# Seams of two attentions and a merge: who stores the last rows, which queues load the first ones, and the first tile in halves

## The chip, the cores and the metric

The kernel runs on one core of a Trainium2 chip. The time is device microseconds of one execution. TensorE (PE) multiplies, VectorE (DVE), ScalarE (ACT) and GpSimd (POOL) do the elementwise work, SyncE (SP) issues DMAs; ACT and POOL can issue them too.

## The reference

One block of an encoder, for 2048 tokens of width 1024, all in float32:

```
proj = x @ w_in                       # A: q k v, B: q k v, two gates
oa = swa_sink_attention(rope(aq), rope(ak), av, sinks)   # window of 2 chunks of 64, sink in the denominator
ob = diff_attention(rope(bq), rope(bk), bv, lam)         # (p1 - lam * p2) @ v, block-causal
ob = rms_norm(ob per head) * subln_g * (1 - lambda_init)
mix = (sig(gA) * (oa @ w_proj_a) + sig(gB) * (ob @ w_proj_b)) @ w_out
x = layer_norm(alpha * x + mix, ln1_g, ln1_b)
x = layer_norm(alpha * x + moe(x), ln2_g, ln2_b)         # 32 experts, 2 for each token
```

## The kernel before

The program is a row of phases: projection, differential attention (prefix `b_`, writes `ob`), window attention (`a_`, writes `oa`), merge (`m_`, writes `x1` and `acc`), routing, experts, final norm. Each phase has its own semaphores, and ends with a barrier of all engines; `Phase.__exit__` (L69) clears the semaphores and then has a second barrier. Lines L72 and L76 in the profile are these two. Nothing of a phase runs before the one ahead of it has ended on every engine. A product of two float32 matrices is made from high and low parts: ACT copies the high part, VectorE (or POOL) subtracts it to get the low part, and TensorE makes three products.

*Differential attention.* For each of 4 heads and 16 blocks of 128 queries, ACT scales the result to `parts`, POOL adds its two halves to `o` (L1056) and issues the store to `ob` (L1058). In between, TensorE makes the gates, which ACT stores (L1189). At its end POOL waits for its stores.

*Window attention.* 16 tiles of 128 queries, two units (key heads) each. TensorE makes the scores (L687 to L694), VectorE the maxima, ACT the exponentials, TensorE transposes and multiplies by the values. SP issues all loads in an order written out: `load_qk(0)`, `load_v(0)`, `load_qk(1)`, `load_v(1)`, and then in each tile those of two tiles ahead, with waits where a buffer must be free. `load_qk` has two halves, from `qk_hi` and `qk_lo`. For the first tile, which has no chunk before it, the keys are loaded in two pieces (L596 and L597). Beside all this POOL loads a slice of the merge's weights in each tile (`a_raw`, 512 KB, L666, two buffers), ACT makes its high and POOL its low part, and POOL adds the attention's two halves (L660).

*Merge.* 16 tiles of 128 tokens. SP loads `ln1_g`, `ln1_b`, `subln_g`, then `oin` (the rows of `oa` and `ob`), the gates and x of two tiles, and goes on two tiles ahead. VectorE makes the RMS norm of the `ob` half of `oin` (L1539 to L1547, with a square root on ACT, L1481, whose table has to be loaded first), TensorE transposes `oin` (L1430), ACT and VectorE split it (L1485, L1551), TensorE multiplies by `w_proj_a` (to `psa`) and `w_proj_b` (to `psb`), VectorE multiplies by the gates, POOL adds, TensorE transposes and multiplies by `w_out`. `norm` (L1553 to L1568) makes the layer norm up to (y - mean) / deviation, POOL multiplies by gamma and adds beta (L1518, L1520), and ACT stores the tile twice (L1500, L1501). Work is staged one and two tiles apart, in the order that `step` has for each engine.

## Time and profile before

| | |
|---|---|
| median of 3 runs | 2936.3 us (2932.4 to 2944.07) |
| profiled execution | 2936.18 us |
| its span | 2934.1 us |
| mean granted clock of TensorE | 0.949 |
| busy: PE, DVE, ACT, POOL | 89%, 57%, 38%, 29% |
| differential attention, first to last work | 480.6 to 1205 us |
| window attention | 1211.5 to 1383 us |
| merge | 1384.3 to 1802 us |
| DMAs issued by POOL: differential attention, window attention, experts | 64, 16, 100 |

The profile is of one execution. Busy time is the time in which an engine executed an instruction; a row of the timeline gives the start, the duration, the engine and line, and in brackets how long the engine had been idle and what ended that. Rows with a q behind the engine's name are of its instruction queue: DMA issues, waits, and DRAIN, in which the queue waits for its engine to have ended all that it began. The time from a DMA's issue to its landing is in the DMA view.

### The profile page before, as it was taken

To read this page: it belongs to the slowest core of one execution; us is meant where nothing else is said; L and a number is where in the kernel's file an instruction comes from. 1 tells how busy PE (TensorE), PEld (TensorE's weight loads), DVE (VectorE), ACT (ScalarE), POOL (GpSimd) and SP (SyncE) were. 2 spreads that over 40 slices of the span, in tenths; PEclk is the share of its full clock that TensorE was granted. 3 is DMA by queue.
4 is the path that set the end of the run, shared out by engine and by line. 5 is a ranking of instruction groups with operands and counts; after the bars stand their busy time and mean duration, and the time that the engine had idled before them with its cause. 6 is when DMAs were issued, how large, how long until landed. Compare 5 with 4: busy or idle time off the path is not lost. (4 is left out here: it accounts for less than half of the span.)

```text
span 2934.1 us, 45594 instructions
## 1 busy us (share of the span) xinstructions
PE 2611.3 (89%) x14634; PEld 2251.5 (77%) x14635; DVE 1677.0 (57%) x3050; ACT 1126.5 (38%) x1918; POOL 856.2 (29%) x653
## 2 busy tenths in 40 slices
PE   6999995999999999697899995499999999999970
PEld 5888884888888888687788884278888888888860
DVE  6333333666666666386344443576685557657748
ACT  3111111444454444365111111264574446646533
POOL 0111110101010010144122232155464445446535
PEclk9999997999999999798999998799999999999995
DMA  6344436665565653386333324378797779768846
GB/s 219 129 139 161 139 131 193 191 196 186 187 198 170 216 167 136 101 211 186 128 129 129 129 107 147 121 271 287 238 359 229 222 261 314 237 220 300 315 107 243
DMA packets 282227, 568.51 MB, mean 194 GB/s; under 512 B 44816, under 2 KB 140176, under 8 KB 280080
## 3 DMA queue, kind: packets, MB, share of 16 engines
q1 hardware_dynamic: 191184, 430.90, 43.3%
q0 software_dynamic: 18752, 65.02, 8.9%
q10 hardware_dynamic: 72192, 71.31, 7.2%
q8 instruction: 56, 0.92, 0.1%
q14 instruction: 43, 0.35, 0.0%
HBM read 435.55 MB, written 131.60 MB: 193 GB/s over the span
## 5 line engine op out<-in xcount | busy, mean ns | idle before, releaser
L1982 DVE TENSOR_TENSOR e_wl<-rw_raw,e_wh 128x1024 fp32r<-128x1024 f32 (+1 forms) x288 | 422.6, 1511 | 25.9 <-ACT e_wh L2132 25.9
L2132 ACT ACTIVATE e_wh<-rw_raw 128x1024 fp32r<-128x1024 f32 (+1 forms) x384 | 377.6, 1054 | 4.1 <-PE e_py L2097 4.1
L1982 POOL TENSOR_TENSOR e_wl<-rw_raw,e_wh 128x1024 f32 (+1 forms) x96 | 273.7, 2864 | 72.1 <-ACT e_wh L2132 72.1
L246 PE MATMUL j_pg<-qkv_w_hi,j_xh 128*128 128x512 f32 (+1 forms) x640 | 243.8, 381 | 9.0 <-DVE qkv_w_lo L416 9.0
L248 PE MATMUL j_pg<-qkv_w_lo,j_xh 128*128 128x512 f32 (+1 forms) x640 | 238.1, 372 | 0.0
L247 PE MATMUL j_pg<-qkv_w_hi,j_xl 128*128 128x512 f32 (+1 forms) x640 | 237.4, 371 | 0.0
L2083 PE MATMUL e_p_up<-e_wh,e_xh 128*128 128x256 f32 (+1 forms) x784 | 225.4, 287 | 0.0
L2085 PE MATMUL e_p_up<-e_wl,e_xh 128*128 128x256 f32 (+1 forms) x784 | 221.7, 283 | 0.0
L2084 PE MATMUL e_p_up<-e_wh,e_xl 128*128 128x256 f32 (+1 forms) x784 | 221.6, 283 | 0.0
L1056 POOL TENSOR_TENSOR b_o<-b_parts 128x128 f32<-128x128 f32 x64 | 31.2, 487 | 636.3 <-ACT b_parts L1173 636.3
L1107 PE MATMUL b_pg<-b_g_wh,b_g_xh 128*128 128x512 f32 x512 | 209.1, 408 | 0.7 <-DVE b_g_out L1294 0.7
L1107 PE MATMUL b_pg<-b_g_wl,b_g_xh 128*128 128x512 f32 x512 | 205.1, 401 | 0.0
L1107 PE MATMUL b_pg<-b_g_wh,b_g_xl 128*128 128x512 f32 x512 | 203.7, 398 | 0.0
L1238 DVE TENSOR_SCALAR_CACHE_REDUCE b_sc<-b_s 128x512 f32<-128x512 f32 (+3 forms) x320 | 179.2, 605 | 30.4 <-PE b_s L1079 18.6
L1164 ACT ACTIVATE b_th<-b_t 128x512 fp32r<-128x512 f32 (+3 forms) x160 | 85.4, 534 | 286.0 <-PE b_t L1092 277.3
L314 POOL TENSOR_TENSOR j_turned<-j_by_cos,j_by_sin 128x512 f32<-128x512 f32 x64 | 70.6, 1113 | 393.0 <-DVE j_by_sin L450 345.9
L1279 DVE TENSOR_TENSOR b_tl<-b_t,b_th 128x512 fp32r<-128x512 f32 (+3 forms) x160 | 97.5, 609 | 120.2 <-ACT b_th L1164 120.2
L2095 PE MATMUL e_py<-e_wh,e_hh 128*128 128x512 f32 x392 | 163.1, 416 | 0.0
L445 DVE TENSOR_TENSOR j_by_cos<-j_pg,qkv_cos 128x512 f32<-128x512 f32 x64 | 37.6, 588 | 216.5 <-DMA v_lo<-j_staged 145.8
L2083 PE MATMUL e_p_gate<-e_wh,e_xh 128*128 (+1 forms) x392 | 154.5, 394 | 5.9 <-DVE e_wl L1982 3.1
L1157 ACT ACTIVATE b_sc<-b_sc,b_nb 128x128 f32<-128x128 f32 (+15 forms) x128 | 153.2, 1197 | 6.9 <-DVE b_nb L1249 6.9
L2097 PE MATMUL e_py<-e_wl,e_hh 128*128 128x512 f32 x392 | 154.1, 393 | 0.0
(328 smaller groups left out, 7053.2 us busy)
## 6 DMA issues: line engine op xcount, KB each, us to landing
rw_raw<-w_gate_up SPq DMA_DIRECT2D x256, 512.0 KB, 6.1
rw_raw<-w_down SPq DMA_DIRECT2D x128, 512.0 KB, 8.5
b_g_xh<-xt_hi SPq DMA_DIRECT2D x64, 512.0 KB, 3.7
b_g_xl<-xt_lo SPq DMA_DIRECT2D x64, 512.0 KB, 4.9
gates<-b_g_out ACTq DMA_DIRECT2D x64, 256.0 KB, 5.2
m_gt<-gates SPq DMA_DIRECT2D x16, 1024.0 KB, 8.3
qk_hi<-j_staged ACTq DMA_DIRECT2D x16, 832.0 KB, 4.5
qk_lo<-j_staged ACTq DMA_DIRECT2D x16, 832.0 KB, 6.9
```

What stands on the lines that cost most here:

```text
L246: nc.tensor.matmul(out, xh[:, u, ks], w_hi[:, k, cs], start=(k == 0), stop=False)
L247: nc.tensor.matmul(out, xl[:, u, ks], w_hi[:, k, cs], start=False, stop=False)
L248: last = nc.tensor.matmul(out, xh[:, u, ks], w_lo[:, k, cs], start=False, stop=(k == KD - 1))
L1107: last = nc.tensor.matmul(pg[:], x_side, w_side, start=(q == 0), stop=(q == PASSES - 1))
L1238: nc.vector.tensor_scalar(sc[u][:, m, ks], bank[n % 4][:, 0:ks.stop - ks.start], 1.0, NEG, ALU.mult, ALU.max, accum_out=mx[:, u, m, g:g + ...
L1982: (nc.gpsimd if done is w_lo_pool else nc.vector).tensor_tensor(wl[:, slot(e, s), :], raw[:, s:s + 1, :], f(wh[:, slot(e, s), :]), ALU.sub ...
L2083: nc.tensor.matmul(out[:, 0:js.stop - js.start], xh[:, at], hi, start=(k == 0), stop=False)
L2084: nc.tensor.matmul(out[:, 0:js.stop - js.start], xl[:, at], hi, start=False, stop=False)
L2085: last = nc.tensor.matmul(out[:, 0:js.stop - js.start], xh[:, at], lo, start=False, stop=(k == KD - 1))
L2095: nc.tensor.matmul(py[:, js], hh[:, at], wh[:, n, js], start=(k == 0), stop=False)
L2097: last = nc.tensor.matmul(py[:, js], hh[:, at], wl[:, n, js], start=False, stop=(k == KF - 1))
L2132: nc.scalar.activation(wh[:, slot(e, s), :], raw[:, s:s + 1, :], ACT.Copy).then_inc(w_hi, 1)
```

## The change

There are four places.

1. In the differential attention the last of the 64 stores to `ob` is issued by SP, on a semaphore of its own, and not by POOL.
2. In the window attention the loads of the first tile's q and k are issued from two queues: the `qk_hi` half by SP, the `qk_lo` half by ACT, keys ahead of queries and the pieces needed for it ahead of the stand-in piece. The sinks are loaded behind them. POOL waits for the first scores before it loads the first slice of the weights.
3. In the merge SP loads the first `oin` first, then `subln_g`, the gates, the second `oin` and gates, x, and last gamma and beta. The first tile goes in halves: the `oa` half is transposed and split before the norm of the `ob` half is ready.
4. In the last tile of the merge VectorE does gamma and beta in two operations, with the subtraction of the mean and the product with the reciprocal deviation folded in; POOL does nothing for it.

```diff
@@ window attention
+        def first_qk(eng, half, src):
+            rows = slice(half * HD, (half + 1) * HD)
+            for dst, ksrc in ((kh, qk_hi), (kl, qk_lo)):
+                k = ksrc[4].rearrange("(g p) n -> p g n", g=A_KV)
+                eng.dma_start(f(dst[rows, 0, :, CHUNK:W]), k[:, :, 0:P]).then_inc(qk_loaded[0], 16)
+                eng.dma_start(f(dst[rows, 0, :, 0:CHUNK]), k[:, :, 0:CHUNK]).then_inc(stand_in, 16)
+            eng.dma_start(f(qs[rows, 0]), src[0:4, :, 0:P].rearrange("c (b p) n -> p (c b) n", b=2)).then_inc(qk_loaded[0], 16)
...
-            load_qk(0)
+            first_qk(sp, 0, qk_hi)
+            sp.dma_start(sink[:], sinks.rearrange("a (g h) -> a g h", g=A_KV).to_broadcast([P, A_KV, GH])).then_inc(sink_in, 16)
             sp.wait_ge(v_zeroed, 1)
...
             for n, (w, k) in enumerate(w_slices):
+                if n == 0:
+                    pool.wait_ge(scores, 1)
...
+            first_qk(act, 1, qk_lo)
             exps(0)
@@ differential attention
+            sp.wait_ge(added, NQ * B_HEADS)
+            sp.dma_start(ob[SEQ - P:, B_V - BV:], o[:, (NQ - 1) % 2, :]).then_inc(last_stored, 16)
+            sp.wait_ge(last_stored, 16)
...
-                    pool.wait_ge(added, k + 1)
-                    pool.dma_start(ob[i * P:(i + 1) * P, h * BV:(h + 1) * BV], o[:, i % 2, :]).then_inc(stored[i % 2], 16)
+                    if k < NQ * B_HEADS - 1:
+                        pool.wait_ge(added, k + 1)
+                        pool.dma_start(ob[i * P:(i + 1) * P, h * BV:(h + 1) * BV], o[:, i % 2, :]).then_inc(stored[i % 2], 16)
@@ merge
+            load_o(0, 0)
+            sp.dma_start(sg[:], subln_g.to_broadcast([P, BV])).then_inc(sg_in, 16)
+            load_g(0, 0)
+            load_o(1, 1)
+            load_g(1, 1)
+            load_x(0, 0)
+            load_x(1, 1)
+            for src, dst in ((ln_g, gam), (ln_b, bet)):
+                sp.dma_start(dst[:], src.to_broadcast([P, D])).then_inc(vec_in, 16)
...
+            pe.wait_ge(oin_in[0], 32)
+            turn(oin[:, 0, :], first_turned, range(0, KA))
             pe.wait_ge(normed, 1)
-            turn(oin[:, 0, :], ab_turned)
+            turn(oin[:, 0, :], ab_turned, range(KA, KD))
...
                     product(psa, abh, abl, range(0, KA), 0, a_done)
+                    if first:
+                        pe.wait_ge(ab_lo, 1)
...
+            act.wait_ge(first_turned, 1)
+            nc.scalar.activation(abh[:, 0:A_Q], pt[:, 0:A_Q], ACT.Copy).then_inc(first_hi, 1)
             root(0)
-            high_ab(0)
+            act.wait_ge(ab_turned, 1)
+            nc.scalar.activation(abh[:, A_Q:], pt[:, A_Q:], ACT.Copy).then_inc(ab_hi, 1)
...
+                if isinstance(t, int) and t == 0:
+                    dve.wait_ge(first_hi, 1)
+                    nc.vector.tensor_tensor(abl[:, 0:A_Q], pt[:, 0:A_Q], f(abh[:, 0:A_Q]), ALU.subtract).then_inc(first_lo, 1)
                 dve.wait_ge(rooted, t + 1)
...
-                nc.vector.tensor_scalar(y[:, u, :], y[:, u, :], mv[:, 0:1], rs[:], ALU.subtract, ALU.mult).then_inc(centred, 1)
+                if isinstance(t, int) and t == NT - 1:
+                    dve.wait_ge(vec_in, 32)
+                    nc.vector.scalar_tensor_tensor(y[:, u, :], y[:, u, :], mv[:, 0:1], gam[:], ALU.subtract, ALU.mult).then_inc(centred, 1)
+                    dve.wait_ge(centred, NT)
+                    nc.vector.scalar_tensor_tensor(y[:, u, :], y[:, u, :], rs[:], bet[:], ALU.mult, ALU.add).then_inc(affine, 1)
```

How the instructions stand. SP at the start of the window attention, before; `a_qs` are the queries, `a_kh` and `a_kl` the keys' high and low parts, `64x2x64` the stand-in piece:

```order
L584 DMA a_sink<-sinks 128x8
L592 DMA a_qs<-qk_hi 64x8x128
L596 DMA a_kh<-qk_hi 64x2x64
L597 DMA a_kh<-qk_hi 64x2x128
L596 DMA a_kl<-qk_lo 64x2x64
L597 DMA a_kl<-qk_lo 64x2x128
L592 DMA a_qs<-qk_lo 64x8x128
L596 DMA a_kh<-qk_hi 64x2x64
L597 DMA a_kh<-qk_hi 64x2x128
L596 DMA a_kl<-qk_lo 64x2x64
L597 DMA a_kl<-qk_lo 64x2x128
L611 DMA a_vz<-v_hi 64x2x64 x2
```

and now, SP again:

```order
L583 DMA a_kh<-qk_hi 64x2x128
L584 DMA a_kh<-qk_hi 64x2x64
L583 DMA a_kl<-qk_lo 64x2x128
L584 DMA a_kl<-qk_lo 64x2x64
L585 DMA a_qs<-qk_hi 64x8x128
L621 DMA a_sink<-sinks 128x8
L613 DMA a_vz<-v_hi 64x2x64 x2
```

SP has five of the ten loads left, and ACT has the other five ahead of its first exponential:

```order
L583 DMA a_kh<-qk_hi 64x2x128
L584 DMA a_kh<-qk_hi 64x2x64
L583 DMA a_kl<-qk_lo 64x2x128
L584 DMA a_kl<-qk_lo 64x2x64
L585 DMA a_qs<-qk_lo 64x8x128
L751 ACTIVATE a_pr,a_sums<-a_s,a_nb 128x192 x4
```

SP at the start of the merge, before:

```order
L1393 DMA m_gam<-ln_g 128x1024
L1393 DMA m_bet<-ln_b 128x1024
L1394 DMA m_sg<-subln_g 128x128
L1397 DMA m_oin<-oa 128x512
L1398 DMA m_oin<-ob 128x512
L1401 DMA m_gt<-gates 128x2048
L1404 DMA m_xin<-x 128x1024
```

and now:

```order
L1405 DMA m_oin<-oa 128x512
L1406 DMA m_oin<-ob 128x512
L1429 DMA m_sg<-subln_g 128x128
L1409 DMA m_gt<-gates 128x2048
L1405 DMA m_oin<-oa 128x512
L1406 DMA m_oin<-ob 128x512
L1409 DMA m_gt<-gates 128x2048
L1412 DMA m_xin<-x 128x1024 x2
L1436 DMA m_gam<-ln_g 128x1024
L1436 DMA m_bet<-ln_b 128x1024
```

The first `oin` stands first, and gamma and beta stand last. ACT at the start of the merge, now; before, the table load stood ahead of everything and the copy was one of 1024 columns behind the root `m_rt`:

```order
L1524 ACTIVATE m_abh<-m_pt 128x512
L1501 ACT_TABLE_LOAD
L1501 ACTIVATE m_rt<-m_ss,m_eps 128x4
L1527 ACTIVATE m_abh<-m_pt 128x512
L1501 ACTIVATE m_rt<-m_ss,m_eps 128x4
```

The copy of the first half stands ahead of the table load, and that of the second behind the root.

## Rows read from the trace of the kernel before

**Rows 1.** The page: busy time by engine, and TensorE's granted clock in 40 slices.

```profile
PE 2611.3 (89%) x14634; PEld 2251.5 (77%) x14635; DVE 1677.0 (57%) x3050; ACT 1126.5 (38%) x1918; POOL 856.2 (29%) x653
...
PEclk9999997999999999798999998799999999999995
```

**Rows 2.** Waits, 1190 to 1240 us: engine, line, for whom; total, times, longest.

```profile
PE a_s L687 <- DMA a_kl<-qk_lo: 23.1, 1, 23.1
```

**Rows 3.** Waits, 1384 to 1416 us.

```profile
PE m_pt L1430 <- DVE m_oin L1547: 16.7, 1, 16.7
```

**Rows 4.** Timeline of POOL, end of the differential attention: start, duration, what.

```profile
1202.01 0.45 POOL L1056 TENSOR_TENSOR b_o<-b_parts 128x128 f32<-128x128 f32 x1 [8.70 <-ACT b_parts L1173]
1202.75 0.56 POOL L1058 DMA_DIRECT2D ob<-b_o  x1 [0.29 <-POOL b_o L1056]
1211.48 0.95 POOL L638 MEMSET a_vz<- 128x1024 f32 x1 [8.17 <-POOLq L76]
```

**Rows 5.** The barrier's line L72 there: duration in ns, start in us.

```profile
L72 ACTq DRAIN  x1: 8/8/8, 1205.1 to 1205.1; - x1
...
L72 POOLq DRAIN  x1: 5291/5291/5291, 1205.3 to 1205.3; - x1
```

**Rows 6.** Timeline of POOL, end of the window attention.

```profile
1368.73 0.57 POOL L666 DMA_DIRECT2D a_raw<-w_out  x1
...
1379.89 1.40 POOL L660 TENSOR_TENSOR a_o<-a_parts 128x256 f32<-128x256 f32 x2
```

**Rows 7.** The barrier's line L72, end of the window attention.

```profile
L72 POOLq DRAIN  x1: 2674/2674/2674, 1380.0 to 1380.0; - x1
```

**Rows 8.** The same line, end of the expert phase.

```profile
L72 POOLq DRAIN  x1: 5045/5045/5045, 2854.7 to 2854.7; - x1
```

**Rows 9.** Timeline of SP, start of the window attention: two of its issues.

```profile
1217.79 0.61 SPq L597 DMA_DIRECT2D a_kl<-qk_lo  x1
...
1225.60 0.61 SPq L599 DMA_DIRECT2D a_kl<-qk_lo  x1
```

**Rows 10.** Timeline of TensorE: first score group and third.

```profile
1224.46 0.50 PE L687 MATMUL a_s<-a_mask 128*128 128x192 f32 x1 [23.10 <-DMA a_kl<-qk_lo]
...
1231.70 0.50 PE L687 MATMUL a_s<-a_mask 128*128 128x192 f32 x1
```

**Rows 11.** Loads issued at 1211.85, 1215.12 and 1225.60: KB each, us to landing.

```profile
a_qs<-qk_hi SPq DMA_DIRECT2D x1, 256.0 KB, 3.8
...
a_qs<-qk_lo SPq DMA_DIRECT2D x1, 256.0 KB, 7.3
...
a_kl<-qk_lo SPq DMA_DIRECT2D x1, 96.0 KB, 4.1
```

**Rows 12.** Timeline of SP, start of the merge: its first issue.

```profile
1384.38 0.34 SPq L1393 DMA_DIRECT2D m_gam<-ln_g  x1
```

**Rows 13.** Timeline of VectorE, start of the merge.

```profile
1392.48 0.69 DVE L1539 TENSOR_TENSOR m_pb<-m_oin 128x512 f32<-128x512 f32 x1 [1.16 <-DMA m_oin<-ob]
```

**Rows 14.** Timeline of ACT, start of the merge.

```profile
1391.50 1.28 ACT L1481 ACT_TABLE_LOAD   x1 [14.01 <-DVE m_sg L1530]
...
1397.94 1.02 ACT L1485 ACTIVATE m_abh<-m_pt 128x1024 fp32r<-128x1024 f32 x1 [3.72 <-PE m_pt L1430]
```

**Rows 15.** Timeline of TensorE, start of the merge.

```profile
1395.94 1.97 PE L1430 MATMUL m_pt<-ident,m_oin 128*128 128x128 f32 x8 [16.70 <-DVE m_oin L1547]
1400.28 0.80 PE L1437 MATMUL m_psa<-mw_w_hi,m_abh 128*128 128x512 f32 x1 [2.37 <-DVE m_abl L1551]
```

**Rows 16.** The load of tile 2, issued at 1398.3: KB, us to landing.

```profile
m_oin<-ob SPq DMA_DIRECT2D x1, 256.0 KB, 4.2
```

**Rows 17.** Timelines of VectorE and ACT, end of the merge.

```profile
1792.16 0.81 DVE L1568 TENSOR_SCALAR m_y<-m_y,m_mv,m_rs 128x1024 f32<-128x1024 f32 x1
...
1797.84 0.34 ACTq L1500 DMA_DIRECT2D x<-m_y  x1
```

**Rows 18.** Groups by form, 1100 to 1200 us: count, total us, mean ns.

```profile
L1271 DVE SCALAR_TENSOR_TENSOR b_at<-b_sc,b_coef 128x512 f32<-128x512 f32 x18 | 14.2, 787 | 0.2
```

More of the change, by code:

```diff
@@ L1427, in _, with turn @@
         def _(pe):
-            def turn(src, done):
-                for k in range(KD):
+            def turn(src, done, ks=range(KD)):
+                for k in ks:
                     last = nc.tensor.transpose(pt[:, k * P:(k + 1) * P], src[:, k * P:(k + 1) * P], ident[:])
@@ L1442, in step @@
             def step(t, k, u):
-                if is_tile(t):
+                first = isinstance(t, int) and t == 0
+                if first:
+                    pe.wait_ge(first_lo, 1)
+                elif is_tile(t):
                     pe.wait_ge(ab_lo, t + 1)
@@ L1453, in step @@
                     product(psa, abh, abl, range(0, KA), 0, a_done)
+                    if first:
+                        pe.wait_ge(ab_lo, 1)
                     if is_tile(t - 1):
@@ L1512, in _ @@
             nc.gpsimd.memset(eps_x[:], EPS / (ALPHA * ALPHA)).then_inc(vec_step, 1)
-            pool.wait_ge(vec_in, 48)
+            pool.wait_ge(vec_in, 32)
             def step(t, k, u):
-                if is_tile(t - 2):
+                if is_tile(t - 2) and not (isinstance(t, int) and t - 2 == NT - 1):
                     pool.wait_ge(centred, t - 1)
```

27 lines of the change are left out of this document (10 added, 17 removed).

## The prediction

> **What bounds the kernel now.** The page comes first: TensorE is busy 89% of the span, at a granted clock of nine tenths or more in nearly every slice [rows 1]. So what can be won without less arithmetic lies where TensorE stands still, and the view of waits shows two such places in the stretches that the change touches: 23.1 us between the second attention's last product and the window attention's first score, put down to the landing of `a_kl` [rows 2], and 16.7 us before the merge's first transpose, put down to VectorE's norm of `m_oin` [rows 3]. Each phase ends in a barrier of all engines, so nothing of the next phase runs under the end of the last one: what a seam loses is lost to the whole, and what it wins is kept, if the phase behind it doesn't wait on something else. I read each seam in the timeline from its last work to the first work behind it, and ask which arrival comes last.
>
> **End of the differential attention.** POOL adds the last block at 1202.01 to 1202.46 and issues its store at 1202.75; the next phase starts at 1211.48 [rows 4]. What lies between is in the queue rows: ACT is done at 1205.1, POOL begins its DRAIN at 1205.3, so the store had landed within 2.5 us of its issue, and the DRAIN lasts 5.29 us, to 1210.6 [rows 5]. The barrier waits for that DRAIN alone. From its end to the new phase's first work it takes 0.9 us. The change moves this one store to SP. SP sees the sum at 1202.5 and gets the same 2.5 us, so is done by 1205.0; ACT's 1205.1 is then last, and the gain is 1210.6 - 1205.15 = 5.4 us, if POOL's DRAIN ends before. Whether it does, the trace of before doesn't show directly, so I bound it. POOL now reaches its DRAIN at about 1202.6. The nearest rows: at the end of the window attention POOL's last DMA was issued at 1368.73, its arithmetic ends at 1381.29 [rows 6], its DRAIN at 1380.0 + 2.67 = 1382.67 [rows 7], 1.4 us behind the arithmetic. At the end of the expert phase the wait ahead of the DRAIN is for POOL's own last scatter, and there the DRAIN takes 5.05 us [rows 8]. So it is long where a DMA of POOL has just landed (two rows) and short where it is 12 us old (one row). Here POOL's last DMA would be the store of the block before, about 10 us old (issued near 1192.8, one block of 10 us earlier). I take the short one: 1202.46 + 1.4 = 1203.9, hidden under ACT. If it keeps its 5.3 us from 1202.6, it ends at 1207.9 and the gain is 2.7 us. The ends of the range are 5.5 and 0 us.
>
> **Start of the window attention.** Call the phase's start T0 (1211.46). SP issues a load each 0.65 us (twelve from 1217.79 to 1225.60 [rows 9]); the last that the first scores need starts at T0+6.3, and the first score at 1224.46, T0+13.0 [rows 10]. So that load took 6.6 us to land. The loads of the first half, issued before POOL's two 512 KB weight loads, land in 3.8 us (the 256 KB `a_qs`); the same load of the second half, issued just behind them, takes 7.3 [rows 11]. After the change five loads go out on SP and five on ACT, the last at T0+2.6 on both, and the weight loads wait for the first scores. I give the last pair 4.1 us, what a load of tile 1 takes with others beside it [rows 11]: T0+6.7, which is 6.3 us earlier. What is late next: the third score group starts 7.24 us behind the first (1224.46 to 1231.70 [rows 10]), so it could start at T0+13.9. Its loads are the next six on SP, behind the sinks and six loads of v: the last is issued at 5 x 0.65 + 0.4 + 6 x 0.65 + 5 x 0.65 = T0+10.8 and lands 4.1 later, T0+14.9, against T0+20.2 now. Between the two I take T0+14.6: the phase gains 5.6 us, and 0.7 of the first 6.3 turns into this new wait. The weight loads now start near T0+10.8, in the same microseconds; only loads issued behind them were slowed, and those are v of tile 1 and q, k of tile 2, which are needed later. Their own first use by ACT lies some 12 us behind, more than the 7.3 us that the slowest load here took. SP's copy of the five moved issues is paid by ACT, which has nothing to do until the first maxima. Bounds: 3.2 us (only five issues saved, landings as slow as now) and 6.3.
>
> The Trainium skill, page "DMA: Bandwidth & Descriptors", section "Issuing engines are not separate DMA queues", speaks against a larger gain: all issuing engines end on the same 16 DMA engines, so issuing on two at once saves only the sequencers' issue time, "which is usually small relative to the DMA itself". The trace says that here it isn't small (the ten issues take half of T0 to T0+13), and what it would give alone is the lower bound, a rival below.
>
> **Start of the merge.** T1 is 1384.3; SP's first issue, `m_gam`, stands at 1384.38 [rows 12]. The first tile's rows of `ob` are the fifth load, behind 1.1 MB, and VectorE starts on them at 1392.48, T1+8.2 [rows 13]. After the change they are the second load, issued at T1+0.5. Landing: 4.2 us for the load of tile 2 beside other traffic [rows 16]; with nothing ahead but 256 KB I take 2.6 to 3. `m_sg` goes third at T1+0.95 and is the later one, T1+3.7. VectorE then starts squaring at T1+3.9 and has the sums at T1+5.4. Meanwhile TensorE transposes the `oa` half: eight take 1.97 us, so four take 1.0 [rows 15], T1+4.1; ACT copies 1024 columns in 1.02 [rows 14], so 512 in 0.6: T1+4.75. Now the table load of 1.28 us [rows 14], which before lay in the wait for the loads, stands behind this copy: T1+6.05. The square root waits for it, 0.65 us more than its input needs, and VectorE's low half (0.68) fits into that gap. Root, reciprocal and two products: 2.0 us, T1+8.1. Then four transposes instead of eight, and the products start, since their low half is long there: T1+9.1. Before it is 1400.28, T1+16.0 [rows 15]. Gain 6.9 us: 4.3 by earlier data, minus 0.7 by the table, 3.3 because four transposes, the copy and the subtraction (1395.94 to 1400.28) are no longer all ahead. The second half needs T1+10.4, and the first product group takes some 7 us from T1+9.1, so it hides. Gates, x, `m_gam` and `m_bet` come later in the queue; some 5 MB land by about T1+16, and their first reader needs them then. With `ob` at 4.2 us the gain is 6.0; with both at 2.2 us it is 7.4.
>
> **End of the merge.** The last tile: VectorE's centring at 1792.16, then two POOL operations, the store at 1797.84 [rows 17]: 5.68 us. Now two SCALAR_TENSOR_TENSOR on VectorE. 512 columns take 0.79 us [rows 18]; by the ratio of an ordinary operation (half of 1024 costs rather more than half) I take 1.35 for 1024, 2.75 for both, gain 2.9 us (bounds 2.5, at twice 0.79 each, and 3.2).
>
> **Sum.** 5.4 + 5.6 + 6.9 + 2.9 = 20.8 us. The profiled execution took 2936.2 us, with a span of 2934.1; that is the median shown, 2936.3, within 0.1. So 2915.5 us. Moving the sinks behind, splitting q and k by half and the new waits of POOL and VectorE on the vectors cost nothing: all they wait for lands before, as reckoned above; without that cover the cost is the lateness itself.
>
> **Rivals.**
> - *The DRAIN stays long.* It may be work for all software DMAs of the phase, 64 of them there and only 16 in the window attention, 5.29 against 1.4 us: nearly the ratio of 4. Then 63 cost as much as 64, and the gain at this place is 2.7: 2918.2. Against it: the expert phase with its hundred has 5.05, not 8.3. Chance 0.27.
> - *The second queue gives its issue time only* (the skill's rule), or SP's stream sets the window attention's pace at once: the phase gains 3.2, not 5.6: 2917.9. For it: the 0.65 us issues fill most of SP's time in a tile. Against: with nothing else in flight the first loads landed in 3.8 us. Chance 0.12.
> - *Several terms at their lower ends* (2.7 + 3.2 + 5.5 + 2.5 = 13.9): 2922.3, which is no change by measurement. Chance 0.13.
> - *Slower.* TensorE rests less: about 12 instead of 23 us and 9 instead of 17 with a few transposes in it. If the clock that it is granted afterwards falls for that, each hundredth costs 27.5 us (2611 x 0.01 / 0.949). The mean granted clock is 0.949; from 0.941 on the gain is gone, and from 0.936 the kernel is slower by over 0.5%: about 2957 at 0.934. Against it: the row of clocks shows the lows at the slices with rests and nine tenths in the long stretches without any [rows 1]. Chance 0.03.
>
> **How the numbers follow.** The forecast, 2915.5, has 0.45 and its own range 2912 to 2918. A change of 0.5% (14.7 us) is about what a measurement tells from none. Faster by more: the forecast, the two middle rivals, together 0.84; within: 0.13; slower: 0.03. The range for 8 in 10 takes in the DRAIN and the queue, and the spread of the runs: 2910 to 2922.
>
> **What would show it.** POOL's DRAIN at that seam under 2 us and its start near 1202.6; the first score 12 to 13 us behind the last product of the differential attention; a wait of under 1 us before the third score group; the first merge product 9 us behind the barrier, with the table load between copy and root; the store of the last tile 2.8 us behind the centring's start. It would be wrong if the DRAIN ends after 1207, if the loads of the first tile on ACT take as long as their issue on SP, or if the span behind the merge grows.

## The result, and the profile after

The changed kernel takes 2921.2 us (median of 5 runs, 2916.4 to 2925.5) against 2936.3: a ratio of 0.9947 with an interval of 0.9927 to 0.9966. Measured again, it gave 2921.7 (6 runs) and 0.9938 [0.9917, 0.9960]. So it is faster by 0.5 to 0.6%, some 15 to 18 us, where 20.8 was forecast. The profiled execution, on which the rows below rest, took 2925.5 us, the slowest of its runs.

The barriers cut the program into phases, and each one's last event on SyncE dates it. These lengths, in us, are the measure of everything below:

| kernel | differential att. | window att. | merge | experts |
|---|---|---|---|---|
| before | 730.9 | 172.9 | 418.5 | 964.7 |
| before, profiled again | 730.7 | 176.0 | 419.0 | 964.8 |
| after | 727.6 | 171.4 | 411.6 | 964.7 |
| after, profiled again | 727.5 | 170.2 | 410.5 | 964.8 |

Means: 3.2 us gained in the first, 3.7 in the second, 7.7 in the third. The phase of the experts, whose code is the same, repeats within 0.1 here; the window attention moves by 3 us with nothing changed. The other two look steadier in these four profiles than they are: later profiles with the changed kernel's code there have 726.9 to 728.6 us in the first and 410.5 to 412.4 in the third. The page of after shows the same busy time as [rows 1] and hardly another clock:

```profile
PE 2612.6 (89%) x14634; PEld 2252.9 (77%) x14635; DVE 1679.7 (57%) x3052; ACT 1126.4 (39%) x1919; POOL 850.6 (29%) x650
...
PEclk9999997999999999798999998699999999999995
```

**End of the differential attention.** First the timeline of POOL and SyncE (start, duration, what), then the barrier's line L72, as in [rows 4, 5]:

```profile
1202.40 0.45 POOL L1066 TENSOR_TENSOR b_o<-b_parts 128x128 f32<-128x128 f32 x1 [8.71 <-ACT b_parts L1184]
1202.87 0.35 SPq L1049 DMA_DIRECT2D ob<-b_o  x1
1209.04 0.96 POOL L641 MEMSET a_vz<- 128x1024 f32 x1 [6.20 <-POOLq L76]
```

```profile
L72 POOLq DRAIN  x1: 5515/5515/5515, 1202.6 to 1202.6; - x1
L72 SPq COMPARE_BRANCH  x1: 43/43/43, 1205.2 to 1205.2; - x1
L72 SPq DRAIN  x1: 7/7/7, 1205.4 to 1205.4; - x1
...
L72 ACTq DRAIN  x1: 8/8/8, 1205.7 to 1205.7; - x1
```

The store on SyncE behaves as reckoned: SyncE and ScalarE are through by 1205.7. But POOL's DRAIN lasts 5.5 us although POOL's last DMA is 9 us old, and ends at 1208.1. The seam, from the end of the last sum to the next phase's first work, is 6.2 us instead of 9.0, in both pairs of profiles.

**Start of the window attention** (T0 = 1209.03). TensorE's first and third score group, as in [rows 10]:

```profile
1216.69 0.50 PE L692 MATMUL a_s<-a_mask 128*128 128x192 f32 x1 [14.94 <-DMA a_qs<-qk_lo]
...
1225.38 0.53 PE L692 MATMUL a_s<-a_mask 128*128 128x192 f32 x1 [1.57 <-DMA a_kl<-qk_lo]
```

The first score comes at T0+7.7 instead of 13.0, the third group at T0+16.4 instead of 20.2, both later than forecast (6.7 and 14.6). The loads behind them, issued at 1211.93 and 1220.10, took 4.6 and 5.2 us to land where 4.1 was reckoned [rows 11]. In the second profile they took 4.8 and 3.5, and the third group started at 15.1 without a wait:

```profile
a_qs<-qk_lo ACTq DMA_DIRECT2D x1, 256.0 KB, 4.6
```

```profile
a_kl<-qk_lo SPq DMA_DIRECT2D x1, 96.0 KB, 5.2
```

**Start of the merge** (T1 = 1380.4). VectorE's first work and TensorE's first turn and product, as in [rows 13, 15], and the two loads that they wait for:

```profile
1385.86 0.23 DVE L1553 TENSOR_SCALAR m_sg<-m_sg 128x128 f32<-128x128 f32 x1 [9.76 <-DMA m_sg<-subln_g]
1385.70 1.12 PE L1443 MATMUL m_pt<-ident,m_oin 128*128 128x128 f32 x4 [10.33 <-DMA m_oin<-ob]
1390.78 1.11 PE L1443 MATMUL m_pt<-ident,m_oin 128*128 128x128 f32 x4 [3.96 <-DVE m_oin L1573]
```

```profile
m_oin<-ob SPq DMA_DIRECT2D x1, 256.0 KB, 4.8
m_sg<-subln_g SPq DMA_DIRECT2D x1, 64.0 KB, 4.5
```

The first product starts at 1391.54, T1+11.1 (forecast 9.1, before 16.0). Nearly all of the 2.0 us are landing time: VectorE's first square starts at T1+5.7 where 3.9 was reckoned, behind loads that took 4.8 and 4.5 us with little ahead, where I took 2.6 to 3 and had 4.2 as a bound [rows 16]. The table load stands between copy and square root, as forecast. At the **end of the merge** the two operations take 1.28 us each and the store is issued 2.64 us behind the centring's start, against 5.68 [rows 17]: 3.0 us, forecast 2.9.

```profile
1784.29 1.28 DVE L1597 SCALAR_TENSOR_TENSOR m_y<-m_y,m_mv,m_gam 128x1024 f32<-128x1024 f32 x1
1785.61 1.28 DVE L1599 SCALAR_TENSOR_TENSOR m_y<-m_y,m_rs,m_bet 128x1024 f32<-128x1024 f32 x1
1786.93 0.34 ACTq L1520 DMA_DIRECT2D x<-m_y  x1
```

### The profile page after: what moved, and what is told of

The parts are those of the page before. It is cut to its first block and busy times, and to the rows that moved or that the text cites. A ratio compares the mean times of both kernels' runs of the same rounds, so it can differ in the third digit from the quotient of the medians.

```text
span 2923.6 us, 45597 instructions
## 1 busy us (share of the span) xinstructions
PE 2612.6 (89%) x14634; PEld 2252.9 (77%) x14635; DVE 1679.7 (57%) x3052; ACT 1126.4 (39%) x1919; POOL 850.6 (29%) x650
## 5 line engine op out<-in xcount | busy, mean ns | idle before, releaser
L1249 DVE TENSOR_SCALAR_CACHE_REDUCE b_sc<-b_s 128x512 f32<-128x512 f32 (+3 forms) x320 | 179.2, 605 | 30.4 <-PE b_s L1090 18.6
```

The lines of the kernel that those rows point to most:

```text
L1249: nc.vector.tensor_scalar(sc[u][:, m, ks], bank[n % 4][:, 0:ks.stop - ks.start], 1.0, NEG, ALU.mult, ALU.max, accum_out=mx[:, u, m, g:g + ...
```

## The experiments

Three things were open: what the DRAIN's length goes by; why the window attention gives back part of its early start, and moves by 3 us by itself; and what sets the landing of the merge's first loads. My theories: the DRAIN counts the software DMAs of the phase (those that GpSimd issues are called so here); SyncE's stream of 13 issues per tile holds TensorE. The rivals: the DRAIN is a fixed price or goes by the age of the last DMA; the clock takes the gain back; loads issued behind slow those ahead. As barriers part the phases, one kernel can carry an edit in each.

### The same two kernels again

> The changed kernel once more, unedited, for the spread of the phase lengths from one profile to the next. Every theory expects the same: differential attention 727.6 us, window attention 171.4, merge 411.6, each within about 1 us; GpSimd's DRAIN at the end of the differential attention 5.5 us again, since no theory makes it a matter of chance; the first score 7.7 us behind the barrier; the merge's first product 11.1 us behind its barrier. If a phase whose code nobody touched moves by more than 1 us, a difference of that size says nothing in a changed one.

> The kernel before once more, for the spread of its phase lengths. Differential attention 730.9 us with a DRAIN of 5.3 us on GpSimd, merge 418.5 us with the first product 16.0 us behind the barrier, each within 1 us. The window attention is the open one. If its length goes by where the spells of half clock fall, it moves by several us from one profile to the next (172.9 before; the changed kernel gave 171.4 and 170.2, two kernels with the same first loads 166.0 and 165.1), while the first score stays at 13.0 us behind the barrier. If the edits of the weight loads made the 166.0 and 165.1, it stays within 1 us of 172.9.

Measured: the lengths of the table above; DRAINs of 5.52 and 5.29 us; first products at 11.0 and 16.4 us; first scores at 12.5 us behind the barrier in before. The window attention of before came out at 176.0 instead of 172.9, so it does move by itself. Of the changed kernel the phase of the differential attention came out at 727.5, the merge at 410.5. In the total the unchanged kernel gave 2942.0 against 2938.4, a ratio of 1.0019 [1.0002, 1.0036]: differences of 0.2% in the medians mean nothing here.

### 15 software DMAs, early weight loads, early table

```
+ ScalarE, block k:  if 1 <= k <= 48: wait added >= k; store block k-1
- GpSimd:  if k < 63: store block k
+ GpSimd:  if 48 <= k < 63: store block k
- GpSimd, window attention:  pool.wait_ge(scores, 1)     # ahead of the weight loads
+ ScalarE, merge:  activation(spare, ident[:, 0:1], Sqrt)  # ahead of all
```

> Three edits in three phases that barriers keep apart. (1) ScalarE stores blocks 0 to 47 of the differential attention, GpSimd only 48 to 62: 15 software DMAs instead of 63, the last one as old as before. If the DRAIN's length goes by the number of software DMAs of the phase, it is here as short as in the window attention with its 16, 1.5 us or less, and the phase ends with ScalarE and SyncE near 724.5 + 0.7 = 725.2 us instead of 727.6, unless the 48 issues slow ScalarE. If it is a fixed price of having used them at all, it stays at 5.3 to 5.5 us and the phase at 727.6. (2) GpSimd's two 512 KB weight loads no longer wait for the first scores. If holding them back made the first loads land sooner, the first score comes 2 to 3 us later, 10 us behind the barrier instead of 7.7; if the gain was only that of the issues on two queues, it stays at 7.7. (3) ScalarE loads the table for the square root while it waits for the first rows of the merge: the first product 0.7 us earlier, 10.4 us behind the barrier instead of 11.1. If the returned clock is fixed by the moment when TensorE starts to work without rests, the merge gets 0.5 to 0.7 shorter; if the clock comes later by as much, less than 0.3.

Measured: 2920.0 us, 0.9938 [0.9916, 0.9959]. (1) The barrier's line and POOL's next work:

```profile
L72 POOLq DRAIN  x1: 1502/1502/1502, 1202.9 to 1202.9; - x1
```

```profile
1207.01 0.96 POOL L641 MEMSET a_vz<- 128x1024 f32 x1 [3.93 <-POOLq L76]
```

The number decides. The seam is 3.9 us (forecast for a short DRAIN: 3.6). The phase takes 726.4, not 725.2: its inside, from the barrier to the last sum, was 1.1 us longer than in after. Among profiles with the changed kernel's code there it lies between 720.7 and 722.5, so the seam is the surer measure. (2) The first score came at 8.3 us, not 10. With the loads held back it came at 7.6 to 8.4 in seven profiles, so what holding them back is worth can't be told from nothing, and isn't 2 to 3 us. (3) The norm's weights landed at 7.9 us behind the barrier, and the first product came at 12.6 instead of 10.4. Whether that was the table load, a later run tells. The window attention took 166.0 us here, 5 less than in the changed kernel, with the same waits for `a_kl` (13.8 us). In the medians, 2920.0 against 2921.2 and 2921.7, these 5 us don't show, so I take them for the spread of that phase from run to run, which isn't shown. They are not in the waits: TensorE stands still for 30.4 us of the phase, 28.9 in after. They are in the work, 135.6 us instead of 142.5 for the same 1088 matmuls, at a granted clock of 0.89 instead of 0.85:

```profile
1206.90:1372.90 166.00, 135.59 (x1088) 132.76 (x1088) 125.69 (x289) 98.72 (x368) 71.79 (x75) 0.89 0.75 191
```

### No software DMA, late weight loads, a held queue

```
+ ScalarE stores blocks 0 to 62
- GpSimd:  pool.wait_ge(scores, 1)
+ GpSimd:  pool.wait_ge(qk_loaded[1], 6 * 16)
+ SyncE, merge, behind the load of sg:  wait oin_in[0] >= 32; wait sg_in >= 16
```

> Three edits in three phases. (1) ScalarE stores all blocks 0 to 62 of the differential attention: no software DMA in it at all. Both theories of the DRAIN (by number, or a fixed price of having used them) expect under 1 us here, and the phase ends with ScalarE and SyncE: 725.2 us. If the DRAIN stays at 5.5 us, software DMAs have nothing to do with it. (2) GpSimd's two weight loads wait until the six loads for the third score group have landed. If the weight loads slow the last of these (it took 5.2 us where 4.1 was reckoned), the third score group starts 1 us earlier, 15.3 us behind the barrier instead of 16.3; if SyncE's pace of issue sets it, it stays at 16.3. (3) In the merge SyncE waits until the first rows and the norm's weights have landed before it issues the gates and all later loads. If the later loads slow the ones ahead of them (4.8 us where 2.6 to 3 was reckoned), the first rows are there 1.5 to 2 us sooner and the first product starts at 9.3 to 9.6 us behind the barrier instead of 11.1; if a load of this shape takes 4.8 us by itself, it stays at 11.1. The gates then come some 4 us later, 10 to 12 us behind the barrier, still ahead of their first reader.

Measured: 2917.9 us, 0.9930 [0.9898, 0.9962].

```profile
L72 POOLq DRAIN  x1: 43/43/43, 1201.0 to 1201.0; - x1
```

(1) Both theories, as expected. The seam is 4.5 us, 0.6 longer than with 48 stores on ScalarE; ScalarE is through with its waits as early as there, and the rest lies in the barrier's own steps. (2) The third score group started at 14.9 us, its last load having landed in 3.3. That would speak for the weight loads as what slows it, if after were the only one to compare with (16.4 and 5.2). But the unedited kernel's second profile has 15.1 and 3.5, and others with its code there 3.4 to 5.2: the landing moves by itself, and the weight loads aren't shown to have a part in it. The phase took 165.1 us, with 11.7 us of waits for `a_kl`. (3) The later loads don't slow the first: with nothing issued behind them, `ob` and the norm's weights were there at 5.2 and 5.4 us, as in after. The merge, 410.8, is no shorter.

```profile
1375.05 1.12 PE L1449 MATMUL m_pt<-ident,m_oin 128*128 128x128 f32 x4 [10.35 <-DMA m_oin<-ob]
1375.20 0.23 DVE L1559 TENSOR_SCALAR m_sg<-m_sg 128x128 f32<-128x128 f32 x1 [9.78 <-DMA m_sg<-subln_g]
```

### 31 software DMAs, one queue, the first tile whole

```
+ ScalarE stores blocks 0 to 31, GpSimd 32 to 62
- ScalarE:  first_qk(act, 1, qk_lo)
+ SyncE:    first_qk(sp, 0, qk_hi); first_qk(sp, 1, qk_lo)
  merge: turn, copy and split of tile 0 whole; last tile through GpSimd as before
```

> Three edits in three phases. (1) ScalarE stores blocks 0 to 31 of the differential attention, GpSimd 32 to 62: 31 software DMAs. By the number theory the DRAIN takes about half of 5.5, 2.7 us; by the fixed price 5.3 to 5.5. (2) The ten first loads of the window attention stand all on SyncE, in the changed order, the weight loads held back as in the changed kernel: the ten issues take 6.5 us instead of 3.2, so the first score starts at about 10 to 10.5 us behind the barrier instead of 7.7. If what an early first score wins is given back by the clock that TensorE is granted, the phase stays within 0.5 us of 171.4; if every microsecond at the start counts, it takes 173.5 to 174. (3) The merge's first tile is turned, copied and split whole, with the loads in the changed order, and the last tile goes through GpSimd's two vector operations again. First product at 11.1 + 3.3 = 14.4 us behind the barrier, last centring to store 5.7 us instead of 2.6: the merge takes 411.6 + 3.3 + 3.0 = 417.9 us, or 1 us less if the clock returns sooner after a later start.

Measured: 2930.0 us, 0.9967 [0.9946, 0.9988].

```profile
L72 POOLq DRAIN  x1: 2815/2815/2815, 1201.0 to 1201.0; - x1
```

(1) 2.8 us, by the number. (2) The first score came at 9.5 us, the third group at 21.3, behind a wait of 4.6 us:

```profile
1214.61 0.50 PE L693 MATMUL a_s<-a_mask 128*128 128x192 f32 x1 [14.50 <-DMA a_qs<-qk_lo]
...
1226.36 0.53 PE L693 MATMUL a_s<-a_mask 128*128 128x192 f32 x1 [4.63 <-DMA a_kl<-qk_lo]
```

The phase takes 176.3, not 171.4 to 174 and no less than before's 172.9 and 176.0, with 18.7 us of waits for `a_kl`. So the order of the loads alone brings an earlier first score, and in this profile nothing of it is left at the third group already, which before had at 20.3 and 19.8; against the changed kernel's two profiles the second queue is worth 1.6 to 1.8 us at the first score and 4.9 to 6.2 at the third group. (3) The first product at 13.2, not 14.4: whole, the table load lies beside VectorE's sums. From VectorE's first square to the first product it takes 7.8 us here as in before, and 5.4 in after. So of the 4.9 us the halves bring 2.4, table load included, and the earlier data 2.5. The merge takes 416.4, 5.4 more than the mean of after's two.

### Dummy work for the clock

```
+ TensorE, window attention:  30 x transpose(tp, ident)   # ahead of the first wait for loads
+ TensorE, merge:  20 x transpose(psb, ident) ahead of, 16 x behind the first turn
+ ScalarE stores blocks 0 to 62
```

> Dummy work is added: TensorE turns the identity matrix 30 times before the first scores of the window attention, 20 times before the first turn of the merge and 16 times between its two first turns, each time into a buffer that is overwritten later. ScalarE stores blocks 0 to 62 of the differential attention, as in the run before with no software DMA there: 724.6 us. If the granted clock comes back when TensorE has been busy for a while, whatever with, it is high from about the first score on in the window attention (before: 19.5 us after it) and from the merge's first product on (before: 5 us after it): the phases get 3 to 5 us and 2 to 2.5 us shorter, 166 and 408.5 to 409. If the clock follows something that dummy work doesn't change, both stay: 170 to 171 and 410.5 to 411.6, though the spells of half clock later in the window attention can move it by some us either way, so the clock's rows at the start decide, not the length alone.

Measured: 2927.1 us, 0.9948 [0.9925, 0.9970]; window attention 168.1, merge 411.0. Stretches of the window attention (busy time of each engine, granted clock, DMA share):

```profile
1207.00:1216.00 9.00, 5.50 (x27) 5.50 (x28) 0.56 (x1) 0.00 (x0) 2.47 (x11) 0.51 0.59 134
1216.00:1222.00 6.00, 4.15 (x39) 4.01 (x36) 2.99 (x9) 2.01 (x11) 1.33 (x2) 1.00 0.91 228
1224.00:1232.00 8.00, 8.00 (x40) 8.00 (x39) 4.08 (x13) 3.56 (x14) 0.00 (x0) 0.50 0.84 152
```

The dummy turns, which waited for the mask and began 3.9 us behind the barrier, do bring the full clock, 2.4 GHz, at the first scores. TensorE then runs out of scores to compute, rests 1.9 us for ScalarE, and is back at half. They also pushed the first score from 7.7 to 9.7 us. Of the 3 to 5 us nothing is left that these lengths can tell. In the merge TensorE was at full clock at the first product, 11.0 us behind the barrier, fell to half within a microsecond, and had the full clock back at 15.2, in after at 16.3; the phase is 411.0, not 408.5 to 409. The clock can be had earlier, but it isn't kept.

### The low halves of v on ScalarE, ob first

```
- SyncE, window attention, tiles from 2 on:  3 loads of v_lo
+ ScalarE, behind copies(2t+1):  wait pv >= 2t; 3 loads of v_lo of tile t+1
- SyncE, merge:  oa, ob, sg, ...
+ SyncE, merge:  ob, oa, ...     ScalarE: sg first
+ ScalarE stores blocks 0 to 62
```

> ScalarE stores blocks 0 to 62 of the differential attention: 724.6 us again. In the window attention ScalarE also issues the three loads of v's low half of each tile from tile 2 on, so that SyncE has 10 instead of 13 issues per tile, 6.5 instead of 8.5 us. If SyncE's stream of issues is what makes TensorE wait for q and k in nearly every tile (10 waits, 12 to 13 us in sum, beside the first), these fall to under 4 us and the phase by 6 to 9 us, to 162 to 165, less what ScalarE's 2 us of issues cost. If it is the landing time of the loads, the waits stay near 12 us and the phase at 170 to 171 within the clock's spread. In the merge the rows of ob go first on SyncE and the norm's weights first on ScalarE, oa second: if the place in the queue sets the landing, the first squares start at 4.9 instead of 5.7 us and the first product at 10.3 instead of 11.1; if these loads land when they land, 11.1.

Measured: 2919.4 us, 0.9932 [0.9915, 0.9948]; window attention 167.9. TensorE's waits in it:

```profile
PE a_s L694 <- DMA a_kl<-qk_lo: 6.9, 8, 1.9
PE a_tp L711 <- DVE a_tcl L822: 5.9, 7, 2.3
```

The waits for q and k are halved, not under 4 us, and a new one, for VectorE's split behind ScalarE's copies, takes their place. The three loads and the wait ahead of them now stand in ScalarE's order ahead of the next tile's copies; that they cause the new wait is read from the order, not tried. In the merge `ob` landed in 4.2 us, but `oa`, now second, in 6.3 and the weights in 5.9; the first product came at 12.7 and the phase takes 413.3. By this one profile the order among the three is not what makes them land sooner.

### The low halves of q and k on ScalarE, early table again

```
- SyncE, window attention, tiles from 2 on:  qs, kh, kl of the low half (qk_lo rows)
+ ScalarE, behind exps(2t+1):  the same three loads of tile t+2
+ ScalarE, merge:  activation(spare, ident[:, 0:1], Sqrt)
+ ScalarE stores blocks 0 to 62
```

> ScalarE stores blocks 0 to 62 of the differential attention: 724.6 us again. In the window attention ScalarE issues the three loads of the low halves of q and k of each tile from tile 2 on, behind its exponentials of the tile two before; SyncE has 10 issues per tile instead of 13. If the number of issues on SyncE is all, the waits for q and k fall to under 4 us as with v's loads. If the moment of the last issue of q and k decides, ScalarE, which comes to it 3 us after the scores and needs 2 us for three, is no earlier than SyncE was: waits near 12 us again, phase 168 to 172. The merge has the early table load once more: its loads are those of the changed kernel. If the late landing of the norm's weights in the first such run (7.9 us behind the barrier instead of 5.3) came from the table load beside it, it comes again and the first product starts at 12.6; if it was chance, they land at 5.3 and the first product starts at 10.4.

Measured: 2912.7 us, 0.9912 [0.9896, 0.9929]; window attention 156.5, merge 411.0. My doubt about ScalarE's lateness was wrong. The simple count was nearer, though it had the waits under 4 us:

```profile
PE a_s L694 <- DMA a_kl<-qk_lo: 5.4, 8, 1.3
PE a_tp L711 <- DVE a_tcl L822: 2.1, 2, 1.2
```

The weights landed in 4.7 us with the table load beside them, so the late landing of the first such run didn't come from it. The first product came at 10.3 us as expected, 4.4 us behind the first square instead of 5.4, yet the merge is as long as with 11.0.

The differential attention, 724.6 us expected as in the first run without a software DMA, took 725.3 us in the run with dummy work and 727.0 in the two behind it. The seam is the same 4.5 us in all four and the DRAIN 0.04; what moved is the inside of the phase.

### That edit alone, with the new start and with the old

```
  changed kernel + the loads of q's and k's low halves on ScalarE
```

> The changed kernel with one edit: from tile 2 on ScalarE issues the three loads of the low halves of q and k of each tile. Nothing else is touched, so the differential attention (727.5 us, DRAIN 5.5) and the merge (410.5 to 411.6) stay. If SyncE's stream of 13 issues per tile was what held TensorE back in the window attention, that phase takes 156 to 159 us here as in the run before, and the total is 2909 to 2912 with runs that lie close together. If the 156.5 us came from where the spells of half clock fell, it takes 165 to 171 and the total is 2917 to 2922.

```
  the same, and the window attention's start as in the kernel before:
- SyncE / ScalarE:  first_qk(sp, 0, qk_hi) / first_qk(act, 1, qk_lo); then sinks
+ SyncE:  sinks; load_qk(0)   # eleven loads
- GpSimd:  pool.wait_ge(scores, 1)
```

> The same edit of ScalarE's loads, but the start of the window attention as in the kernel before: all twelve first loads on SyncE, the weight loads not held back. Differential attention and merge are the changed kernel's. The first score comes 13.0 us behind the barrier instead of 7.7. If the change's gain at the start was given back only because the stream of issues on SyncE was the bound behind it, all of it counts here: the phase takes 5.3 us more than with the new start, 162 us. If the gain at the start is lost whatever the stream does, for instance to the clock, it takes at most 2 us more.

Measured: 2910.7 us, 0.9900 [0.9885, 0.9915], phase 157.9; and with the old start 2916.1, 0.9929 [0.9915, 0.9943], phase 161.0. Their first score groups:

```profile
1217.30 0.50 PE L694 MATMUL a_s<-a_mask 128*128 128x192 f32 x1 [14.79 <-DMA a_qs<-qk_lo]
```

```profile
1221.08 0.50 PE L689 MATMUL a_s<-a_mask 128*128 128x192 f32 x1 [19.54 <-DMA a_kl<-qk_lo]
```

7.6 against 12.3 us behind the barrier, 4.7 apart; the totals stand 5.4 apart, the phases 3.1 in these two profiles. So much of the start is kept, but this doesn't show that the stream had taken it before: with all loads on SyncE a start earlier by 5.0 us in the means made the phase 3.7 shorter, and a share of 0.74 can't be told from one of 0.66 here.

That SyncE has room now shows in its own waits. It waited for TensorE ahead of v's loads for 14.0 us in the changed kernel (first line) and 26.9 in this one:

```profile
SPq L613 <- PE a_o L731: 14.0, 5, 4.2
```

```profile
SPq L615 <- PE a_o L733: 26.9, 14, 4.4
```

The merge, untouched, took 412.4 us in both kernels, not 410.5 to 411.6, with the first product at 12.1 and 12.7 us: the norm's weights took 6.0 and 6.6 us to land, where after had 4.5. The differential attention took 728.6 and 726.9.

### All together

```
  changed kernel + 48 stores on ScalarE + q's and k's low halves on ScalarE + early table
```

> The changed kernel with the three edits that looked good: ScalarE stores blocks 0 to 47 of the differential attention and GpSimd only 15 (seam 2.2 us shorter than the changed kernel's, from the last sum to the next phase's first work 3.9 instead of 6.2), ScalarE issues the low halves of q and k in the window attention (13 us less, if the phase of 156.5 us is repeated; 0 to 5 if it was chance), and the early table load in the merge (first product at 10.3 instead of 11.1 us, phase 0 to 0.7 us less). Sum 2921.5 - 2.2 - 13 - 0.4 = 2906 us; by the rival 2914 to 2919.

Measured: 2912.9 us, 0.9919 [0.9905, 0.9933], not the 2906 expected, though its profile has a span of 2907.0 and the changed phases at or near their shortest: 724.2, 155.2 and 410.4 us. The 5 runs lie between 2908.7 and 2917.7, and the route phase, whose code is untouched, took 96.1 instead of 93.1 us. Against the single edit's 2910.7 neither better nor worse can be told.

```profile
1207.40:1362.60 155.20, 133.64 (x1088) 131.12 (x1088) 124.60 (x289) 99.06 (x368) 71.69 (x75) 0.91 0.84 204
```

Beside it the same stretch of the changed kernel:

```profile
1209.00:1380.40 171.40, 142.49 (x1088) 139.94 (x1088) 125.86 (x289) 98.60 (x368) 71.60 (x75) 0.85 0.72 185
```

The same 1088 matmuls take 133.6 instead of 142.5 us, at a granted clock of 0.91 instead of 0.85, and what TensorE doesn't work falls from 28.9 to 21.6. More than half of the gain is the clock's. It can't be put down to the fewer rests alone: in the run with 15 software DMAs the same matmuls took 135.6 us with 30.4 us of rest.

### Twice the software DMAs

```
- GpSimd:  store block k                       # 128 rows
+ GpSimd:  store rows 0 to 63, store rows 64 to 127 of block k
```

> The changed kernel with one edit: each of GpSimd's 63 stores of the differential attention is issued as two of 64 rows each, so 126 software DMAs carry the same bytes. So far the DRAIN took 0.04 us behind no software DMA, 1.50 behind 15, 2.82 behind 31, 5.52 behind 63: 0.083 us for each more. If it goes by the number of DMAs without limit, it takes 10.7 us here and the phase 732.9 instead of 727.6. If it goes by the rows (or descriptors) that they carry, it stays at 5.5. If it stops growing somewhere, as the 5.05 us of the expert phase with its hundred suggest, it is between 5 and 6 as well, and which of the two it is stays open. GpSimd's second issue of a block costs 0.6 us of idle time. The window attention and the merge are the changed kernel's: 166 to 172 and 410.5 to 411.6.

```profile
L72 POOLq DRAIN  x1: 10663/10663/10663, 1206.7 to 1206.7; - x1
```

10.7 us and a phase of 732.9, both as the count foretells; the bytes are the same. The window attention took 171.8 and the merge 411.0 (first product at 10.7 us), a third profile of the changed kernel's code in both. The total, 2933.7 us with 0.9978 [0.9961, 0.9994], is 12 above the changed kernel's, and only 5.3 of that are this phase; the rest lies in phases with untouched code (this profile has the first at 485.3 instead of 481.4 and the route phase at 95.6 instead of 93.3), and what lengthens those stays open.

## Why the prediction came out as it did

The time, 2921.2, lies inside the range given and 5.7 us above the forecast, outside the forecast's own 2912 to 2918. By the phases' lengths the gain is 14.6 of 20.8 us. All four places gained, and three of the four terms were too large. What came is nearest to the rival with several terms at their lower ends (13.9 us, 2922.3), which had a chance of 0.13. So the range held because it had been widened for the DRAIN and the queue, not because the forecast's sum was right, and one sign of being wrong did appear: the DRAIN ended behind 1207.

- *End of the differential attention, 5.4: got 2.8 at the seam.* The step that failed is the choice between two prices of the DRAIN. I took it for a matter of the last DMA's age, on three rows; it goes by the number of software DMAs in the phase: 0.04 us behind none, 1.50 behind 15, 2.82 behind 31, 5.52 behind 63, 10.66 behind 126, which is 0.08 us for each more. The rival said exactly this and gave the right 2.7. What I held against it, the expert phase with a hundred and 5.05 us [rows 8], doesn't bear on it as I thought: all but one of those are indirect DMAs, of which no run here tells the price. The 64 of before, with 5.29 us, lie 0.3 under the line through the others; why is open. Where the DRAIN is short, the seam comes near the forecast's 3.6: 3.8 to 4.0 us in the three runs with 15 or 31, and 4.5 in the four with none.
- *Start of the window attention, 5.6: got 3.7 by the means, 1.5 in the first pair of profiles.* What was sized wrong stands at the start itself. The first score came 1.0 us later than reckoned, by a landing of 4.6 us instead of 4.1 and by ScalarE's issues, whose fifth stands at T0+2.9, not 2.6. The third group, for which 5.6 was reckoned, gained 3.9 in the first pair and 4.7 in the second, for landings of 5.2 and 3.5 us. TensorE's later waits for `a_kl`, in nearly every tile, were 9.5 and 12.0 us in the two profiles of before (32.6 and 34.5 in all, less the first), and 13.3 and 12.0 in those of after, so in the means two microseconds went there, less than the two of before differ by. SyncE's stream setting the pace was a rival at 0.12, as something that could limit the gain at the start. That it took back part of the start isn't shown; that it limits the whole phase is: three of the 13 issues, those of q's and k's low halves, moved to ScalarE made it 13 to 16 us shorter, in three kernels. Three loads of v moved instead left as little waiting for `a_kl` (6.9 us) and brought 3 us only, with SyncE waiting 26.1 us for GpSimd and 26.0 for TensorE. So it matters which loads go and where they stand on ScalarE, not their number alone. The profiles of the phase together, in us, with the same 1088 matmuls in each (the run with dummy work has more):

| q's and k's low halves | start | length | TensorE not busy | busy | clock |
|---|---|---|---|---|---|
| SyncE | old (before, twice) | 172.9, 176.0 | 31.0, 32.6 | 141.9, 143.4 | 0.85, 0.84 |
| SyncE | new (three times) | 171.4, 170.2, 171.8 | 28.9, 27.9, 27.7 | 142.5, 142.3, 144.2 | 0.85, 0.86, 0.85 |
| SyncE | new, weight loads early; late | 166.0, 165.1 | 30.4, 27.4 | 135.6, 137.7 | 0.89, 0.88 |
| SyncE | new order, all on SyncE | 176.3 | 36.4 | 139.9 | 0.86 |
| SyncE, v's on ScalarE | new | 167.9 | 26.4 | 141.5 | 0.87 |
| ScalarE | old | 161.0 | 25.9 | 135.2 | 0.88 |
| ScalarE | new (three kernels) | 157.9, 156.5, 155.2 | 23.8, 21.7, 21.6 | 134.1, 134.8, 133.6 | 0.90, 0.89, 0.91 |

So moving the three loads of q and k took off 4 to 7 us of rests and 8 to 9 us of work, this at a higher clock. In after SyncE issues one load behind the other while TensorE has the full clock, a tile in 8.5 us where each issue takes its 0.65, and TensorE waits for it. SyncE's own pauses of over 0.8 us are five between 1221 and 1380, each at or just behind a stretch at half clock (1294.5 to 1297.5, for one, with half clock from 1291 to 1297). One such tile of issues:

```profile
1311.26 0.60 SPq L598 DMA_DIRECT2D a_qs<-qk_hi  x1
...
1319.15 0.53 SPq L618 DMA_DIRECT2D oa<-a_o  x1
1319.73 0.60 SPq L598 DMA_DIRECT2D a_qs<-qk_hi  x1
```

The Trainium skill, page "DMA: Bandwidth & Descriptors", section "Issuing engines are not separate DMA queues", holds that a second issuing engine saves only the sequencer's issue time, usually a small thing. By the trace that time, 13 x 0.65 = 8.5 us of a tile of 8.5 to 9.3, is what bounds this phase where TensorE has the full clock, while the DMA engines were busy for 0.72 of it and carried the shorter one at 0.84.
- *Start of the merge, 6.9: got 4.9 (first product).* The size that was off is the landing: 4.8 us for 256 KB with little ahead, not 2.6 to 3, and it is not the traffic behind that makes it so long. The earlier data brought 2.5 us of the 4.3 reckoned. The halves less the table load brought 2.4 of 2.6; the table load alone costs some 1.0 us, as the run with it out of the way shows, and not 0.65. (The loads that stood ahead of `ob` before are 1.3 MB, not 1.1; no term rests on it.) *Its end, 2.9: got 3.0.* Together the merge is 7.7 us shorter in the means, and 7.2 with all five profiles of the changed merge, in which the first product comes at 10.7 to 12.7 us.
- *The clock* took little over all: in the page its row differs in one digit, and the mean is 0.950 against 0.949. But within the window attention it has a part in the length that wanders. In the middle of the phase it falls to half for some microseconds, at other tiles in each profile. One such stretch of after, behind one at the full clock, with the wait that stands in it:

```profile
1320.00:1328.00 8.00, 6.29 (x57) 6.15 (x56) 7.53 (x19) 5.80 (x23) 3.89 (x5) 1.00 0.77 215
1328.50:1335.00 6.50, 5.61 (x27) 5.61 (x27) 2.32 (x6) 0.60 (x3) 1.44 (x2) 0.50 0.84 215
```

```profile
1329.39 0.53 PE L692 MATMUL a_s<-a_mask 128*128 128x192 f32 x1 [3.10 <-DMA a_kl<-qk_lo]
```

TensorE had rested 3.1 us for a load just as the clock fell. In the four kernels with fewer waits the mean clock of the phase is higher, but also in two with as many waits, as the table shows; that a rest brings each spell was not tried by itself.

What stays open: why early loads of 256 KB land in 3.0 us at one place and in 4.8 at the next; where the spells of half clock fall, and whether the weight loads have a part in the 166.0 and 165.1 us; and the microseconds by which the untouched first and route phases differ between kernels.

## What to carry to other kernels

Before a gain at the start of a phase is booked, look at what each tile behind it waits for: if an engine's issues (here 13 of 0.65 us) fill a tile's time, moving the right three of them can bring more than the whole seam, as here, and moving three others little. Count the direct software DMAs of a phase: at its end GpSimd's DRAIN took 0.08 us for each, however old they were, so let another engine issue them where its queue has room. Half of them was enough here, since the other engines' ends came last from there on. Take the landing time of a first load from a row of its own kind and place, and with two rows take the longer. Before a microsecond is put down to an edit, look at how far the same row moves in the profiles where its code is untouched.

## What the runs showed of the hardware

- The DRAIN of GpSimd's queue grows with the number of direct software DMAs issued before it in its phase, 0.082 us each between 15 and 126, whether they move 64 KB or 32 KB, and though the last has landed long before. The window attention, with 16 of 512 KB, fits if the DRAIN's own part begins where the arithmetic ends, which isn't shown: in after 2.67 us of DRAIN from 1376.1, arithmetic until 1377.4, 1.4 us left against 1.50 behind 15.
- The same 1088 matmuls of a phase took 133.6 to 144.2 us as the mean granted clock went from 0.91 to 0.84. From 171.4 to 155.2 us of length the idle part gave 7.3 us and the busy part 8.9 (these kernels differ at the seam and in the table load too, neither of which touches that phase's matmuls). Two kernels had the higher clock without the fewer rests.
- Dummy turns for 6 us brought the full clock to the first scores; after a rest of 1.9 us it was at half in 1224 to 1232, with TensorE busy for 8.00 of 8.00 us.
